# First unit's weights loaded and split ahead of token blocks 2 and 3; experts' gate and up weights loaded in halves of the inner dimension

## What is computed

```python
h = _rmsnorm(x, norm_mix)
q_a, k_a, v_a, q_g, k_g, v_g, r_g, f_lr, gate_a, gate_b = jnp.split(h @ w_in, _split_points(), axis=-1)
...   # windowed attention -> a_out, gated linear attention -> g_out
merged = jax.nn.sigmoid(gate_a) * (a_out @ w_proj_attn) + jax.nn.sigmoid(gate_b) * (g_out @ w_proj_gla)
x = x + merged @ w_out
x = x + _moe(_rmsnorm(x, norm_ffn), ...)
...
def _moe(h, w_rg, b_rg, w_re, b_re, w_eg, w_eu, w_ed):   # 32 experts in 4 groups, 2 experts for each token
    a = jnp.einsum('nd,edf->nef', hf, w_eg[sl])          # gate: 1024 -> 256
    u = jnp.einsum('nd,edf->nef', hf, w_eu[sl])          # up:   1024 -> 256
    act = jax.nn.silu(a) * u * combine[:, sl, None]
    out = out + jnp.einsum('nef,efd->nd', act, w_ed[sl]) # down: 256 -> 1024
```

## Time and profile before

| | |
|---|---|
| median of 3 runs | 816.71 us (815.89 to 817.4) |
| profiled execution, its own time | 818.9 us |
| profiled execution, span | 817.0 us |
| mean granted clock of TensorE | 0.963 of full |
| PE busy | 727.8 us, 89% of the span |
| weights of the experts | 96 loads of 1 MB on SP's queue |

### The profile page before, as it was taken

The page is one execution under the profiler, slowest core; times in us unless marked ns, Lnnn a source line. Parts: engine busy times, 40 slices in busy tenths (PEclk is TensorE's granted clock), DMA queues, the critical chain, the costliest instruction groups (busy, mean ns, idle before and its releaser), DMA issues.

```text
span 817.0 us, 12277 instructions
## 1 busy us (share of the span) xinstructions
PE 727.8 (89%) x5112; PEld 541.2 (66%) x5112; DVE 340.8 (42%) x623; ACT 244.0 (30%) x489; POOL 82.9 (10%) x138
## 2 busy tenths in 40 slices
PE   3999999999999999999999999999979769878830
PEld 2788997778999998879999978854433223333310
DVE  5463259654565437444355523732223111111128
ACT  6224275454454343333122241301111001010113
POOL 3304000000000100000000011212112111111200
PEclk9999999999999999999999999999989898998975
DMA  8641111113132623523233398759999999999735
GB/s 310 188 136 61 52 53 52 53 52 103 53 99 57 258 79 109 201 68 100 61 95 92 102 377 359 277 189 411 421 423 422 426 421 422 423 412 394 311 139 205
DMA packets 73415, 173.02 MB, mean 212 GB/s; under 512 B 7040, under 2 KB 41184, under 8 KB 65152
## 3 DMA queue, kind: packets, MB, share of 16 engines
q1 hardware_dynamic: 63520, 148.52, 48.1%
q0 software_dynamic: 9840, 23.72, 7.9%
HBM read 163.26 MB, written 18.74 MB: 223 GB/s over the span
## 4 chain that ended last, share of the span: by engine, by line
PE 65%; DMA 21%; DVE 9%; ACT 2%; issue 2%; SPq 1%; POOL 0%; POOLq 0%; ACTq 0%; DVEq 0%
PE bank L723 43%; DMA expert_down<-in_w_exp_down 16%; PE bank L1188 5%; PE bank L1172 4%; DMA expert_gate_up<-in_w_exp_up 2%; DVE w_split L1530 2%; PE bank L743 1%; DMA x_rows<-in_x_prompt 1%; ACT w_split L1226 1%; PE bank L1100 1%; PE bank L1008 1%; DMA token_out<-token_out_scratch 1%; PE bank L1014 1%; DVE s_state L1828 1%; PE bank L959 1%
## 5 line engine op out<-in xcount | busy, mean ns | idle before, releaser
L723 PE MATMUL bank<-hT_split,w_split 128*128 128x272 f32 x1152 | 154.1, 292 | 0.0
L723 PEld LDWEIGHTS bank<-hT_split,w_split 128*128 128x128 f32 x1152 | 147.3, 188 | 2.1 <-issue 0.9
L723 PE MATMUL bank<-w_split,hT_split 128*128 128x512 f32 (+1 forms) x576 | 131.6, 383 | 1.0 <-DVE w_split L1530 1.0
L723 PEld LDWEIGHTS bank<-w_split,hT_split 128*128 128x128 f32 x576 | 101.5, 191 | 24.0 <-issue 3.3
L1172 PE MATMUL bank<-expert_gate_up,gatheredT 128*64 128x512 f32 x512 | 112.9, 593 | 2.9 <-DMA expert_gate_up<-in_w_exp_up 2.0
L1530 DVE TENSOR_TENSOR w_split<-w_raw,w_split 128x2048 fp32r<-128x2048 f32 (+1 forms) x35 | 75.9, 2168 | 82.7 <-ACT w_split L1226 82.7
L1188 PE MATMUL bank<-expert_down,expert_actT 128*64 128x512 f32 x256 | 71.5, 709 | 34.8 <-DMA expert_down<-in_w_exp_down 30.8
L1172 PEld LDWEIGHTS bank<-expert_gate_up,gatheredT 128*64 128x64 f32 x512 | 39.1, 137 | 73.1 <-issue 70.1
L1226 ACT ACTIVATE w_split<-w_raw 128x2048 fp32r<-128x2048 f32 (+1 forms) x35 | 63.5, 1813 | 45.1 <-PE bank L723 17.5
L1188 PEld LDWEIGHTS bank<-expert_down,expert_actT 128*64 128x64 f32 x256 | 21.5, 162 | 74.2 <-issue 41.2
L723 PE MATMUL bank<-gla_outT_split,w_split 128*128 128x272 f32 x384 | 49.4, 288 | 0.0
(11 more groups left out here) (355 smaller groups left out, 840.3 us busy)
## 6 DMA issues: line engine op xcount, KB each, us to landing
expert_gate_up<-in_w_exp_gate SPq DMA_DIRECT2D x32, 1024.0 KB, 18.6
expert_gate_up<-in_w_exp_up SPq DMA_DIRECT2D x32, 1024.0 KB, 20.4
expert_down<-in_w_exp_down SPq DMA_DIRECT2D x32, 1024.0 KB, 19.5
w_raw<-in_w_in SPq DMA_DIRECT2D x15, 1024.0 KB, 5.7
w_raw<-in_w_in SPq DMA_DIRECT2D x16, 512.0 KB, 4.7
s_state<-in_state_gla POOLq DMA_DIRECT2D x4, 1024.0 KB, 9.7
out_sample_gla_state<-s_state POOLq DMA_DIRECT2D x4, 1024.0 KB, 6.0
w_raw<-in_w_proj_gla SPq DMA_DIRECT2D x8, 512.0 KB, 4.3
```

The costliest lines, as they stand in the source:

```text
L723: ins = mm(out, stat(x, k), mov(y, k), start=first and n == 0 and m == 0, stop=last and n == len(ks) - 1 and m == 2)
```

## The change

It has three parts. At the start, SP loads unit 0 between block 1 and blocks 2 and 3; ACT and DVE split unit 0 ahead of the norms of blocks 2 and 3; PE turns block 2 after unit 0's block 0 and no longer before unit 0. For the experts, each load of gate or up is cut in two: `kh` is 0 or 1 for the first or second 4 of the 8 rows that a partition holds (4 KB per partition, 512 KB per load). Each half has its own semaphore for each buffer, PE waits for the second half after 16 of the 32 matmuls, and signals `gu_done` after each half, so that SP can load the first half of a buffer while PE still reads the second. Third, the routing tables lie in another place of the memory, and some semaphores are merged into one (`sq_mm` and `sv_mm` into `s_mm`, `ck_turned` and `sp_turned` into `s_turned`, three for exponentials into `exp_in` and `exp_out`), with the counts to match.

```diff
-    WGU = [at(f"expert_gate_up_{b}", [128, 2, 2, KC, FF], F, off) for b, off in enumerate((D0, D0 + 49152, H0))]
+    WGU = [at(f"expert_gate_up_{b}", [128, 2, 2, 2, KC // 2, FF], F, off) for b, off in enumerate((D0, D0 + 49152, H0))]
...
-            for bl in (1, 2, 3):
-                load_x(bl)
+            load_x(1)
...
             for u in range(NU - 2):
                 next_unit(u)
+                if u == 0:
+                    load_x(2)
+                    load_x(3)
...
-            def load_gate_up(b, experts):
+            def load_gate_up(b, experts, kh):
                 for half, e in enumerate(experts):
                     for m, name in enumerate(("w_exp_gate", "w_exp_up")):
-                        sp.dma_start(WGU[b][:, half, m, :, :].rearrange("p k n -> p (k n)"),
-                                     expert_rows(name, e).rearrange("(p k) n -> p (k n)", k=KC)).then_inc(gate_up_in[b], 16)
+                        sp.dma_start(WGU[b][:, kh, half, m, :, :],
+                                     expert_rows(name, e).rearrange("(p c k) n -> p c k n", c=2, k=KC // 2)[:, kh]).then_inc(gate_up_in[kh][b], 16)
...
                 if n + 1 < 2 * PEELED:
-                    sp.wait_ge(gu_done, n - 1)
-                    load_gate_up((n + 1) % 3, pair(n + 1))
+                    for kh in range(2):
+                        sp.wait_ge(gu_done, 2 * (n - 2) + kh + 1)
+                        load_gate_up((n + 1) % 3, pair(n + 1), kh)
...
-                        if s == 1:
-                            turn_h(3)
+                        if s in (1, 2):
+                            turn_h(s + 1)
...
-            for bl in (4, 0, 1, 2):
+            for bl in (4, 0, 1):
                 turn_h(bl)
...
                 for k in range(KC):
+                    if k == KC // 2:
+                        ins.then_inc(gu_done, 1)
+                        pe.wait_ge(gate_up_in[1][gb], gate_up_count)
...
-            for bl in (4, 0, 1, 2):
+            for bl in (4, 0, 1):
                 square_x(bl)
             ht_hi(4)
             ht_hi(0)
+            split_hi(0)
+            square_x(2)
+            ht_hi(1)
             square_x(3)
-            ht_hi(1)
-            split_hi(0)
             ht_hi(2)
             split_hi(1)
             ht_hi(3)
...
             ht_lo(0)
+            split_lo(0)
             norm_h(2)
             ht_lo(1)
             norm_h(3)
-            split_lo(0)
             ht_lo(2)
+            split_lo(1)
             ht_lo(3)
-            split_lo(1)
```

More of the change, by code:

```diff
@@ L189, in decoder_step @@
     ACTT = [at(f"expert_actT_{u}", [128, 2, 128], F, W0 + 11264 + 1024 * u) for u in range(2)]
-    RR = [at(f"route_{n}", [128, NB, NE], F, W1 + 640 * n) for n in range(5)]
-    PROD = at("route_products", [128, 2, NB, NE], F, W1 + 3200)
-    SELB = at("route_selected", [128, NB, NE], BF, W1 + 4480)
-    PAIRH = at("route_pairs", [128, 2 * NB, NFIX], F, W1 + 4800)
-    OHP = at("slot_pair_digits", [128, 2 * NB, 4, NFIX], BF, W1 + 5440)
-    OHR = at("slot_row_onehot", [128, 2 * NB, 128], BF, W1 + 6720)
+    T0 = W0 + 20480
+    RR = [at(f"route_{n}", [128, NB, NE], F, T0 + 640 * n) for n in range(3)]
+    PROD = at("route_products", [128, 2, NB, NE], F, T0 + 1920)
+    SELB = at("route_selected", [128, NB, NE], BF, T0 + 3200)
+    PAIRH = at("route_pairs", [128, 2 * NB, NFIX], F, T0 + 3520)
+    OHP = at("slot_pair_digits", [128, 2 * NB, 4, NFIX], BF, T0 + 4160)
+    OHR = at("slot_row_onehot", [128, 2 * NB, 128], BF, T0 + 5440)
     V0 = W0 + 13312
@@ L450, in decoder_step @@
         h2_stored, lg_mm, lg_out, half_sums = (sem(n) for n in ("h2_stored", "lg_mm", "lg_out", "half_sums"))
[L451 to L452 removed]
+        sel_ready, rank_mm, rank_read = (sem(n) for n in ("sel_ready", "rank_mm", "rank_read"))
         digits_ready, rows_hot, table_mm, rows_ready = (
@@ L455, in decoder_step @@
         over_hot, over_mm, over_ready, iters_ready = (sem(n) for n in ("over_hot", "over_mm", "over_ready", "iters_ready"))
-        gate_up_in = [sem(f"gate_up_in{b}") for b in range(3)]
+        gate_up_in = [[sem(f"gate_up_in{kh}{b}") for b in range(3)] for kh in range(2)]
         down_in = [sem("down_in0"), sem("down_in1")]
@@ L553, in _ @@
             sp.dma_start(NFFN[:], a["norm_ffn"].partition_broadcast(128).rearrange("p a n -> p (a n)")).then_inc(norm_in, 16)
-            load_gate_up(0, pair(0))
+            for kh in range(2):
+                load_gate_up(0, pair(0), kh)
             load_down(0, pair(0))
-            load_gate_up(1, pair(1))
+            for kh in range(2):
+                load_gate_up(1, pair(1), kh)
             sp.wait_ge(main_mm, unit_done(NU - 1))
             sp.wait_ge(x2_out, 2 * NB)
-            load_gate_up(2, pair(2))
+            for kh in range(2):
+                load_gate_up(2, pair(2), kh)
             sp.wait_ge(rows_ready, 2)
@@ L575, in _ @@
                                              min_val=0, max_val=NE - 1) for half in range(2)]
-                    sp.wait_ge(gu_done, 2 * i + u - 1)
-                    load_gate_up((2 * PEELED + u) % 3, experts)
+                    for kh in range(2):
+                        sp.wait_ge(gu_done, 4 * i + 2 * u - 3 + kh)
+                        load_gate_up((2 * PEELED + u) % 3, experts, kh)
                     sp.wait_ge(dn_done, 2 * i + u - 1)
@@ L1170, in expert_pair @@
                 for k in range(KC):
+                    if k == KC // 2:
+                        ins.then_inc(gu_done, 1)
+                        pe.wait_ge(gate_up_in[1][gb], gate_up_count)
                     for half in range(2):
                         ins = mm(P[2 + u][64 * half:64 * half + 64, :].rearrange("p (m n) -> p m n", m=2),
-                                 XT[u][:, k, 64 * half:64 * half + 64], WGU[gb][:, half, :, k, :], start=(k == 0), stop=(k == KC - 1))
+                                 XT[u][:, k, 64 * half:64 * half + 64], WGU[gb][:, k // 4, half, :, k % 4, :], start=(k == 0), stop=(k == KC - 1))
                 ins.then_inc(gu_done, 1)
@@ L1468, in _ @@
             run_units(range(NU))
-            act.wait_ge(l_exp_in, 1)
-            A(RG[2][:], RG[2][:], ACT.Exp).then_inc(l_exp, 1)
-            act.wait_ge(l_exp_in, 2)
-            A(R1["e2"][:], R1["d"][:], ACT.Exp).then_inc(l_exp, 1)
+            act.wait_ge(exp_in, 2)
+            A(RG[2][:], RG[2][:], ACT.Exp).then_inc(exp_out, 1)
+            act.wait_ge(exp_in, 3)
+            A(R1["e2"][:], R1["d"][:], ACT.Exp).then_inc(exp_out, 1)
             A(DUMMY[:], EPSC[:], ACT.Silu)
```

50 lines of the change are left out of this document (24 added, 26 removed).

## The result

The changed kernel takes **810.18 us** (median of 4 runs, 809.08 to 811.38) against 816.74 us for the kernel before (4 runs, 815.89 to 817.40). The ratio is 0.9922, with a 95% interval of 0.9908 to 0.9937: 6.4 us faster, interval 5.1 to 7.5. The profiled execution had an own time of 809.67 us and a span of 807.8.

The account below looks back on a forecast made before the run. PE was taken as the bound up to about 541 us, then the stream of expert weights on SP's queue. Start -3.4 and experts +0.3 made -3.1 us, from 816.7 to 813.6 us, range 808.8 to 816.8.

Parts of the forecast that it names:

- the first rival: Expert stream: halves cost nothing there, so the total is -7.35 us, at 809.4 us; chance 0.27.
- Part 1, the start: Start: first split matmul at 18.6 us in place of 22.94, less 0.9 for block 2's transposes: -3.4 us.
- The tightest cover: Start: block 3's lower part ends near 30.6 us and PE wants it at about 31.0, 0.4 us of cover.
- The second rival, the clock: Start: the clock rises no earlier, so the start gains only 1.2 us and the total is 815.8 us; chance 0.15.
- Part 2, the gap: Start of the expert stream: the first reload is issued 3.5 us earlier and the DMA gap near 549 us closes: -1.9 us.
- Part 3, the last pair: End of the experts: PE starts pair 15 on its first half without waiting for the last load: -2.05 us.
- Part 4, the price of halves: Expert stream: 512 KB loads run at 409 GB/s, not 425, costing +5.1 us, +4.3 before pair 12's down.
- its sign: Expert stream over 560 to 720 us: about 410 to 415 GB/s would confirm the price of halves; before, 421 to 426.
- Part 5: Merged semaphores and moved routing tables: no wait changes, worth nothing.
- The slow rival: Expert stream: slowed more than all gains, below 393 GB/s; at 390 GB/s the total is 819.1 us; chance 0.06.
- The rival's formula: Whole kernel: the change in us is 0.85x - 7.35, where x is the us that the stream loses.

Follow-up runs that it names:

- experiment 1: The kernel before, unedited, profiled a second time in one run: 815.47 us.
- start_only: The kernel before with only the new order at the start on SP, ACT, DVE and PE: 812.32 us, ratio 0.9952.
- late_release: The changed kernel, but SP waits for PE to finish a whole buffer before loading either half: 812.62 us, ratio 0.9952.
- both_before: The changed kernel, but PE waits for both halves before it starts a pair: 813.14 us, ratio 0.9958.
- experiment 2: Parts alone against the kernel before: new start 812.32 us; new start with SP's old load order 814.08; half loads with old start 813.53.
- quarters_2kb: The changed kernel with each 512 KB load cut into two 256 KB loads over all partitions, in 2 KB pieces: 826.39 us, ratio 1.0127.

## Why the prediction was right, and where its sum was off

The forecast of 813.6 us had the direction and its range held the time. But it was 3.4 us too slow, and took the change for half of its worth. The measured time lies by the first rival, 809.4, and that is luck: the rival says that halves cost nothing in the stream, and they cost nearly 4 us there. All three gains were larger than forecast, and the rival's missing price stands in for them.

**Part 1, the start: predicted -3.4, measured -3.9 [-5.1, -2.6].** The chain was right in its steps and to a tenth: from block 1's landing to the first split matmul it forecast 18.6 - 10.29 = 8.3 us, and the profile has 16.89 - 8.63 = 8.3. The extra turn inside PE's steady stretch costs 0.85 us: from the first split matmul to unit 1 it is 13.06 us after and 12.21 in experiment 1; 0.9 was taken. The tightest cover held too: block 3's lower part ends at 26.8, and PE wants it at 24.22 + 12 x 0.242 = 27.1; 0.4 us of cover was forecast, 0.3 is there. The new place in SP's queue is needed: without it 1.1 us of waiting for the load come back.

**The second rival, the clock, falls.** The 402 ns spacing was read as a property of the start. Experiment 1 shows it as one of that execution: 256 ns in another of the same kernel, 256 and 253 ns in `start_only` and after. The granted clock reads 1.00, the level of 2.4 GHz, over these matmuls in every one of the executions, so the column gives no warning, and that the clock made the 402 ns is not shown. The Trainium skill (TensorE: Matmul & The Clock Gate, Part 1) says that the moment of the rise differs from run to run; the spacing of these matmuls does, and no rise is to be seen.

**Part 2, the gap: predicted -1.9, measured -2.4** by the median of `late_release`, 2.3 by the bytes that are missing there, and 3.0 to 3.5 by the landing of pair 12's down weights. The idle gap is what was forecast: over 540 to 545 us it is 0.69 MB, 1.6 us. What makes the gain larger than that is open.

**Part 3, the last pair: predicted -2.05, measured -2.9** (`both_before`, where PE is idle for 2.66). The 2.05 of the earlier trace rows was again one execution's: the kernel before has 2.65 in its second execution. With whole loads the wait can also bring slower matmuls behind it, 1.7 us in `start_only`, which the sum did not have.

**Part 4, the price of halves, was about right in size and wrong in its reasons.** It took +5.1 us for the stream and +4.3 for the down of pair 12. The landing of that pair's down weights is 3.9 us later with halves when the early release is taken away (199.4 against 195.5). Of the 3.9, 2.3 is the pieces, of which the prediction said "the piece alone costs nothing", and 1.5 is the slow spell at pair 3's reload, which it did not know; a price for each load all along the stream, its own reason, is not to be seen at 512 KB. That the two come to nearly its figure is luck. Three readings went wrong. The earlier trace rows gave 409 GB/s for 512 KB loads in a stretch of 5 us in the output phase, and it was the nearest row in size only: in the experts' stream such loads run at 416 to 418, a little over the 410 to 415 that the prediction named as its sign., 425 and 426 GB/s, were read as "the piece alone costs nothing"; stretches of 4 and 6 us with 2 MB do not tell 1% apart, and over 178 us the piece is more than half of the price. And the price was put down to the small packets at a load's end, which at 512 KB cost nothing visible on a full queue. The runs put in its place: about 5 ns per packet and DMA engine, a slow spell where a buffer is first loaded in halves, and a price per load all along only at 256 KB, the one size under 512 KB tried.

The fixed 2 us that the prediction takes from the Trainium skill (DMA: Bandwidth & Descriptors, Anatomy of one DMA) is the page's figure for transfers that GpSimd issues, while SP issues these loads. No run here shows it for a load by itself.

**Part 5: nothing** up to the experts, by the traces of experiment 2; behind that it is inside the terms above.

**The sum again.** With all terms by the runs, and the two of the stream by the landing of pair 12's down weights, it is -3.9 - 3.2 - 2.9 + 3.9 = -6.1 (-5.3 with the 2.4 of the median for part 2), and the change was measured twice, at -6.4 and -7.5. Against the forecast, 0.5 us more came from the start, 1.3 from the early release, 0.9 from the last pair, and 0.4 from a price that was a little smaller.

**The other side.** The slow rival needed a stream below 393 GB/s. The changed kernel is far from it, but `quarters_2kb` at 391 shows that it exists, one step of the same edit further: 10.4 us slower than the kernel before by the median, and 5.6 in the run that was profiled at 391. The rival's formula gives 2.2 at that speed, so it was too mild.

**The base.** The profiled execution stood 2.2 us over the median, and the prediction carried that offset through. That did no harm to the sum, but the surplus lay in the very stretch that was changed, in a late load and a slow spell of matmuls, and a part of it could have been taken for a gain of the change: the two profiles alone show 7.0 us at pair 0's first matmul (542.55 against 535.52), and 3.2 of it is the execution's.

## What to carry to other kernels

Where a stream of queued loads is the bound, cutting loads buys release and start at the edges of the stream only: cut the first reload and the last load, and leave the middle in the longest contiguous pieces, since each further piece per partition is paid in every load. That was tried here on one kernel. Before a rate is taken from a trace to price 1%, it wants a stretch that is long enough to show 1%, in the same surroundings. When the start of one execution is costed, a second profile of the same kernel tells which of its waits belong to the kernel. And where a price has two possible causes, as pieces and loads here, each wants a kernel of its own; comparing where one and the same load lands settled what the medians could not.

## What the runs showed of the hardware

- Loads over 64 partitions run at 231 to 313 GB/s, while the slices that fit loads over 128 in the same kernel read 372 to 413; with full width, loads of the same 256 KB reach 391. The Trainium skill (DMA: Bandwidth & Descriptors, The descriptor swizzle) says that partitions 0 to 63 and 64 to 127 are written through different halves of the ports. The runs agree, in so far as two such loads in a row do not add up to full speed.
- The queue is full 25 us earlier with halves: issues of over 1 us on SP begin at 555.94 us, 20.4 behind pair 0's first matmul, and before at 587.94, 45.4 behind it. So SP is counted as the chain for 16% of the span where it was 1%, at no cost that shows: over 600 to 700 us the stream moves 418 GB/s, and 419 with whole loads of the same pieces.
- On a full queue, beside gathers and scatters, 512 KB loads move as much as 1 MB loads of the same pieces, 418 against 419 GB/s. At the first reload of a buffer they do not: 309 to 342 GB/s for 5 us, with the DMA engines busy.
- A wait of 3.23 us before pair 15 left the granted clock at 0.50 for a while and 32 matmuls took 8.78 us; after 2.66 us it stayed at 1.00 and they took 7.09.
